# The order of attention's 24 units: a sample ahead of two prompt heads instead of between them

## What is computed

```python
p_c = _attn_probs(q, ckv[:, :, 0], qpos, kpos_c, rel_bias, kpos_c[None, :] <= qpos[:, None])
o_c = jnp.einsum('bhgqk,bkhd->bqhgd', p_c.astype(ckv.dtype), ckv[:, :, 1])
sel = _select_blocks(p_c, qpos, n_slc)
o_s = sel_fn(q, sel)
o_w = win_fn(q)
o = gates[:, :, 0] * o_c + gates[:, :, 1] * o_s + gates[:, :, 2] * o_w
out = o.astype(h.dtype).reshape(B, S, N_HEADS * HEAD_DIM) @ w_o_l
```

## Time and profile before

| | us |
|---|---|
| median of 3 runs | 2566.35 |
| lowest and highest | 2563.49, 2566.51 |
| profiled execution | 2564.04 |
| its span | 2562.5 |
| PE busy in the span | 2506.9 (98%) |
| attention, P0's scores to the first matmul of `w_o` | 1368.02 to 1486.05 |

### The profile page before, as it was taken

How to read it: one execution, slowest core, us unless ns; L and a number is a source line. 1 busy time by engine, 2 the same in 40 slices (tenths; PEclk the granted TensorE clock), 3 DMA queues, 4 the chain that set the end, 5 groups by cost and what they waited for, 6 DMA issues and landing times.

```text
span 2562.5 us, 44071 instructions
## 1 busy us (share of the span) xinstructions
PE 2506.9 (98%) x17354; PEld 2464.4 (96%) x17354; DVE 1203.5 (47%) x1361; ACT 923.7 (36%) x1154; POOL 267.6 (10%) x316
## 2 busy tenths in 40 slices
PE   7999999999999999999999999899999999999997
PEld 7899999999999999899997799899999999999997
DVE  7654444444444444643535743744444444444444
ACT  5554233323323333622325633633333233323332
POOL 0410000000000001300002311300000000000012
PEclk9999999999999999999999999999999999999999
DMA  6434444444444444456445464344544444444443
GB/s 247 177 136 147 151 160 149 151 158 160 151 150 161 147 142 159 142 153 183 157 171 177 154 191 160 106 149 152 167 147 147 151 160 147 149 161 155 151 148 126
DMA packets 89482, 400.66 MB, mean 156 GB/s; under 512 B 13788, under 2 KB 24428, under 8 KB 59858
## 3 DMA queue, kind: packets, MB, share of 16 engines
q1 hardware_dynamic: 77810, 377.82, 43.5%
q0 software_dynamic: 6160, 12.60, 1.5%
q10 hardware_dynamic: 5456, 9.52, 1.0%
HBM read 392.16 MB, written 19.02 MB: 160 GB/s over the span
## 4 chain that ended last, share of the span: by engine, by line
PE 89%; DVE 5%; ACT 3%; issue 1%; DMA 1%; POOL 1%; SPq 0%; ACTq 0%; DVEq 0%
PE ps L1403 28%; PE ps L1405 28%; PE ps L1404 27%; PE ps L1488 2%; ACT w_hi L490 1%; DVE w_lo L820 1%; PE ps L1662 1%; PE ps L1588 1%; ACT y L596 0%; ACT x_hi L514 0%; DMA rowsK<-cmp_data_dram 0%; PE ps L1514 0%; PE ps L1659 0%; POOL sc L1368 0%; PE ps L1692 0%
## 5 line engine op out<-in xcount | busy, mean ns | idle before, releaser
L1403 PE MATMUL ps<-x_hi,w_hi 128*128 128x320 f32 x3536 | 1094.9, 310 | 7.6 <-DVE sg L1037 4.1
L1404 PE MATMUL ps<-x_lo,w_hi 128*128 128x320 f32 x3536 | 1093.3, 309 | 0.0
L1405 PE MATMUL ps<-x_hi,w_lo 128*128 128x320 f32 x3536 | 1093.3, 309 | 0.0
L820 DVE TENSOR_TENSOR w_lo<-w_raw,w_hi 128x2048 fp32r<-128x2048 f32 (+1 forms) x362 | 744.4, 2056 | 646.3 <-ACT w_hi L490 646.3
L490 ACT CAST w_hi<-w_raw 128x2048 fp32r<-128x2048 f32 (+1 forms) x362 | 618.9, 1710 | 507.6 <-PE ps L1405 478.7
L1403 PEld LDWEIGHTS ps<-x_hi,w_hi 128*128 128x128 f32 x3536 | 664.2, 188 | 9.6 <-DVE sg L1037 4.6
L1404 PEld LDWEIGHTS ps<-x_lo,w_hi 128*128 128x128 f32 x3536 | 664.3, 188 | 0.2
L1405 PEld LDWEIGHTS ps<-x_hi,w_lo 128*128 128x128 f32 x3536 | 664.3, 188 | 0.0
L1405 PE MATMUL ps<-hid_hi,w_lo 128*128 128x320 f32 x1408 | 435.1, 309 | 0.0
L1403 PE MATMUL ps<-hid_hi,w_hi 128*128 128x320 f32 x1408 | 435.1, 309 | 0.0
L1404 PE MATMUL ps<-hid_lo,w_hi 128*128 128x320 f32 x1408 | 435.1, 309 | 0.0
(11 more groups left out here) (255 smaller groups left out, 1471.5 us busy)
## 6 DMA issues: line engine op xcount, KB each, us to landing
w_raw<-w_in_dram SPq DMA_DIRECT2D x176, 1024.0 KB, 4.9
w_raw<-w_out_dram SPq DMA_DIRECT2D x128, 704.0 KB, 4.0
w_raw<-w_kv_dram SPq DMA_DIRECT2D x24, 1024.0 KB, 6.8
w_raw<-w_q_dram SPq DMA_DIRECT2D x17, 1024.0 KB, 4.9
w_raw<-w_o_dram SPq DMA_DIRECT2D x15, 1024.0 KB, 5.6
win_out_dram<-win_kv_dram POOLq DMA_DIRECT2D x8, 992.0 KB, 5.2
rowsK<-cmp_data_dram SPq DMA_DIRECT2D x16, 256.0 KB, 9.0
pastK<-slc_k_dram SPq DMA_DIRECT2D x16, 256.0 KB, 3.4
```

Source lines behind the costliest of these rows:

```text
L820: V.tensor_tensor(w_lo[:, slot, 0:width], src, w_hi[:, slot, 0:width].bitcast(F32), ALU.subtract).then_inc(lo_made, 1)
L1403: M(out, wh, xh[:, k, :], start=(k == 0), stop=False)
L1404: M(out, wh, xl[:, k, :], start=False, stop=False)
L1405: last = M(out, wl, xh[:, k, :], start=False, stop=(k == kt - 1))
```

## The change

`unit` and `place` now put a sample first in each trio: S0 P0 P1, S1 P2 P3, and so on to S7 P14 P15. PE starts the first sample's scores right behind the turned values. The matmul of the prompt's compressed keys, with its wait for the GELU, moves behind these scores, the compressed values follow it, and then comes the wait for `kc_made`. DVE copies `kcP` at step 1, ahead of the scores of the first head, so behind the whole of the first sample's scores. Since the first sample's value copy writes a region that the GELU reads, DVE waits there for `cmp_hid`.

```diff
--- before.py
+++ after.py
@@ -302,11 +302,11 @@
     def unit(p):
 
         b, k = divmod(p, 3)
-        return NH + b if k == 1 else 2 * b + k // 2
+        return 2 * b + k - 1 if k else NH + b
 
     def place(u):
 
-        return 3 * (u - NH) + 1 if u >= NH else 3 * (u // 2) + 2 * (u % 2)
+        return 3 * (u - NH) if u >= NH else 3 * (u // 2) + 1 + u % 2
 
     def is_sample(p):
 
@@ -1164,8 +1164,6 @@
 
         crow_copy(1, 0)
         cmp_join(3, 2, NKV, False)
-        dve.wait_ge(kc_sum, 2)
-        V.tensor_copy(kcP[:, :], ps[:, 3, 0:NKV * NCMP]).then_inc(kc_made, 1)
 
 
         def scores_p(p):
@@ -1206,6 +1204,8 @@
                                    in1=rep(bn, 2), op0=ALU.mult, op1=ALU.add)
             link(V.scalar_tensor_tensor(out=o[:, 0:NC4], in0=ps[:, a, W:W + NC4], scalar=SCALE,
                                         in1=biasSC[:, :], op0=ALU.mult, op1=ALU.add))
+            if b == 0:
+                dve.wait_ge(cmp_hid, 4)
             if b >= 2:
                 dve.wait_ge(o_made, place(NH + b - 2) + 1)
             V.tensor_copy(vC[:, b % 2, :], ps[0:NC4, a, 512 - HD:512])
@@ -1250,6 +1250,9 @@
                                 x_hi[:, :, o:o + DS].bitcast(F32), ALU.subtract).then_inc(o_read, 1)
 
         for s in range(UNITS + 4):
+            if s == 1:
+                dve.wait_ge(kc_sum, 2)
+                V.tensor_copy(kcP[:, :], ps[:, 3, 0:NKV * NCMP]).then_inc(kc_made, 1)
             if s < UNITS:
                 scores_s(s) if is_sample(s) else scores_p(s)
             if 1 <= s < UNITS + 1:
@@ -1623,9 +1626,10 @@
         pe.wait_ge(gates_made, 1)
         turn_values(2)
         turn_values(3)
-        pe.wait_ge(cmp_hid, 4)
-        M(ps[:, 3, 0:NKV * NCMP], w2[:, 0, :], hcP[:, 0, :], start=True, stop=True).then_inc(kc_sum, 1)
-        pe.wait_ge(kc_made, 2)
+        def compressed_keys():
+
+            pe.wait_ge(cmp_hid, 4)
+            M(ps[:, 3, 0:NKV * NCMP], w2[:, 0, :], hcP[:, 0, :], start=True, stop=True).then_inc(kc_sum, 1)
 
         def compressed_values():
 
@@ -1745,7 +1749,9 @@
             if s < UNITS:
                 scores(s)
             if s == 0:
+                compressed_keys()
                 compressed_values()
+                pe.wait_ge(kc_made, 2)
             if s == 1:
                 new_values()
             if s == 2:
```

## The result

The changed kernel takes 2569.0 us (median of 20), the kernel before 2564.2 us in the same series; the ratio is 1.0016, with a 95% interval of 1.0009 to 1.0022. So the changed kernel is slower by 0.16%, 4.1 us (2.3 to 5.6), inside what was called no change and inside the range. I therefore measure everything in the stage from the end of the turned values.

The account below looks back on a forecast made before the run. TensorE, busy 98% of the span, was taken as the bound, leaving only fill and drain to change. +0.88 - 0.05 + 1.75 = +2.58 us on a median of 2566.35 gave 2568.9 us, range 2563.7 to 2572.6.

Parts of the forecast that it names:

- The fill: Start to the third unit's scores: TensorE waits about 1.1 us for the key copy queued on VectorE; +0.88 us.
- The middle: Third unit's scores to the 24th's: seven steady trios of 13.667 us, 95.67 against 95.72 us; -0.05 us.
- wait for their keys: Second sample's scores: key transfers land by 1378.4, scores due about 1378.5, covered narrowly; waiting would show the forecast wrong.
- The drain: Last scores to the output projection's first matmul: later cast of the first w_o panel, 17.97 against 16.22 us; +1.75 us.
- The sum: Fill, middle and drain together: +0.88 - 0.05 + 1.75 = +2.58 us.
- The clock: TensorE's granted clock was to stay 1.00 throughout, despite two drain gaps of some 2 us.
- first gap: Drain, TensorE idle 2.2 us ahead of the transposes before the sample's outputs; forecast to lose nothing on the chain.
- the third rival: Clock falls in the drain's first gap and stays at half: +8.9 us in all, 2575.3 us; chance 0.08.
- the last gap: Drain: if the clock falls only there, the projection loses 1.7 us, giving 2570.6 us, within the range.
- A slip in the chances: Faster by more, under 2561.2 us, was said to need all the fill's idles and half as much again; 0.02.
- Rival 1: Drain: split of w_o isn't on the chain, drain 0.4 us shorter; +0.4, 2566.8 us; chance 0.14.
- Rival 2: Fill: keys' wait and the fill's idles disappear, drain stays 16.22 us; -2.2 us, 2564.1 us; chance 0.05.

Follow-up runs that it names:

- e3: Changed kernel with VectorE copying the compressed keys at step 0, ahead of the first sample's softmax; ratio 1.0012 to the kernel before.
- e9: Changed kernel with eight idle products on TensorE in each of the drain's two long gaps; ratio 1.0003 to the kernel before.
- e8: Kernel before with one more wait: ScalarE casts the first w_o panel only when unit 21's outputs are done; ratio 1.0006.
- e1: Changed kernel with VectorE's low part of the first w_o panel moved behind the last unit's copy and unit 21's low part; ratio 0.9999 to the kernel before.
- e11: Kernel before, unchanged, profiled once more for the clock; one execution, stage 128.03 us against 126.38.
- e2: Changed kernel with ScalarE casting the first w_o panel ahead of the last sample's row copy; ratio 1.0005 to the kernel before.
- e4: Changed kernel with the compressed keys finished ahead of the first unit again, only the unit order new; ratio 1.0025 to the kernel before.
- e7: Kernel before with VectorE's low part of the first w_o panel behind the last unit's copy and unit 21's output; ratio 0.9999.
- e5: Changed kernel with eight idle products on TensorE in the drain's second gap, ahead of the last outputs; ratio 1.0005 to the kernel before.
- e6: Changed kernel with early keys' copy, low part behind the last copy, and eight idle products in the drain's first gap; ratio 0.9995 to the kernel before.
- e12: Kernel before with the low part behind the last copy and six idle products in the fill's 1.72 us gap; ratio 0.9989.

## Why the prediction was right, and where it was off

- **The fill, +0.88**: measured 7.79 - 7.04 = +0.75. The gap at the new wait was forecast at 1.1 us and was 1.06, ended by the copy of the keys. e3 shows that it was that copy's place.
- **The middle, -0.05**: from the third unit's scores to the last's 95.82 us (103.61 - 7.79 from the turned values), against 95.72 (102.76 - 7.04): +0.1. The trio stayed at 13.67 us, and the second sample's scores did not wait for their keys (they started at 1380.95, or 1378.5 on the prediction's scale, which is when they were said to be due).
- **The drain, +1.75**: 17.85 - 16.22 = +1.63 at full clock (e9). The cast was forecast at +9.36 and came at +9.38. e8 shows that a late cast alone, 1.30 us later, makes the old order's drain longer by as much, e1 that the low part ahead of the last copy is what hands it on.
- **The sum, +2.58**: +2.47 at full clock (e9 against before).
- **The clock**: here the working was off. The granted clock was said to stay at 1.00, and a fall in the drain was one of the prediction's own signs of being wrong; it came. I took the fill's gap of 1.72 us as one that leaves the clock alone, from a single execution; e8 and e11 fell behind just that gap. So the old order isn't free of it, and in the new one the clock fell behind the first gap in 3 of 7 profiles, where the third rival had a chance of 0.08. The third rival's place was right (e1, e2 and e4 fell behind the first gap), its size wasn't: the clock did not stay at half (in e1 it was 0.51 from 1477.5 to 1480.5 and 1.00 from 1481 to 1485), and it cost 1.58 us in place of 6.3; in e4, where it fell behind both gaps, 2.92 in all. Behind the last gap I had 1.7 us and in the two profiles of the changed kernel it was 2.5, since the last outputs slow down as well (0.45 us, 18.30 against 17.85) and the panel loses 2.05 (9.45 against 7.40).
- **The Trainium skill's sentence** on transposes ("TensorE: Matmul & The Clock Gate", Part 4: PE-mode transpose), that they don't count as busy TensorE as matmuls do, would have had the clock fall behind the first gap. It did in 3 of 7 profiles and not in 4, with the same gap and the same transposes behind it; whether transposes count less, no run here separates.
- **Rival 1** (the split not on the chain) falls by e1. **Rival 2** (the keys' wait disappears) falls: the wait was there, one engine further on.

- **A slip in the chances**: 5.1 us are 2.3 times the fill's idles of 2.23 us, not one and a half times; nothing else hangs on it.

So the size came out right for the chain, and the remaining 1.6 us of the measured 4.1 are a term that I had left to a rival. The interval of the difference (2.3 to 5.6 us) takes in the chain alone, so it is the profiles and not the times that show this term. That the forecast median, 2568.9 us, is within 0.1 us of the measured 2569.0 is luck: it stood on a median of three runs, 2566.35, where the kernel before had 2564.2 in the series that counts, and the price was too small by about as much.

## What to carry to other kernels

Rotating the units of a pipeline leaves its steady period alone; what changes is the fill and the drain, and these can be worked out to 0.15 us here by walking each engine's written order from rows of the same unit in the same neighbourhood. Look there for work of the next stage (a cast, a split) that sits ahead of the last unit's own steps: it cost 0.7 us where what it waits for came early (e7) and 2.4 us where it came late. And before calling a gap of the matmul engine harmless to its clock, take profiles of more than one execution.

## What the runs showed of the hardware

The granted clock fell to 1.2 GHz behind gaps of 1.71 (e8), 1.72, 2.14 and 2.19 us of an otherwise busy TensorE, in some executions and not in others, of the same kernel; it cost 1.3 to 2.5 us each time. Idle products that left 0.2 to 0.4 us of such a gap were followed by no fall in the profiles of the four kernels that had them (e5, e6, e9, e12), one profile each, and cost the chain nothing.
